# A decoder trunk layer on one core: the way from x to the first matrix product, written another way

## What is computed

```python
h = rmsnorm(x, norm_mix_g)          # x * rsqrt(mean(x*x) + eps) * g, over 2048 channels
p = h @ w_in                        # 2048 x 5120, columns [u_A | v_A | B_gate | C_gate | x_B]
v = rmsnorm(gelu(p[..., o1:o2]), sgu_norm_g)
y_a = gelu(p[..., :o1]) * chunk_sgu(v, w_s, b_s)
y_b = B_gate * causal_dwconv3(C_gate * x_B)
x = x + concat(GroupRMSNorm(y_a), GroupRMSNorm(y_b)) @ w_out
x = x + (silu(causal_dwconv3(h2 @ w_gate)) * (h2 @ w_up)) @ w_down    # h2 = rmsnorm(x)
```

## Time and profile before

| | |
|---|---|
| median of 3 runs | 2396.19 us (2394.45 to 2396.49) |
| the profiled execution | 2393.88 us, span 2392.2 us |
| PE busy in the span | 2339.3 us (98%) |
| DVE, ACT, POOL busy | 1331.8, 809.9, 269.0 us |
| first matmul of the first product | 34.99 us after the span's start |

### The profile page before, as it was taken

The page is one execution under the profiler, slowest core; times in us unless marked ns, Lnnn a source line. Parts: engine busy times, 40 slices in busy tenths (PEclk is TensorE's granted clock), DMA queues, the critical chain, the costliest instruction groups (busy, mean ns, idle before and its releaser), DMA issues.

```text
span 2392.2 us, 42851 instructions
## 1 busy us (share of the span) xinstructions
PE 2339.3 (98%) x17506; PEld 2328.4 (97%) x17506; DVE 1331.8 (56%) x1639; ACT 809.9 (34%) x1036; POOL 269.0 (11%) x362
## 2 busy tenths in 40 slices
PE   6999999999999899999999999999999999999996
PEld 5999999999999899999999999999999999999996
DVE  5347754455322767778778778778773222222332
ACT  6224322213111444444444444444442111111222
POOL 4310000000322000111111111111111000000111
PEclk7999999999999999999999999999999999999998
DMA  4522232323433233443443443443448543342222
GB/s 147 180 72 73 71 88 74 88 76 120 154 101 102 83 99 108 135 126 101 133 125 102 133 125 103 131 125 105 129 157 282 178 139 125 122 149 99 79 76 84
DMA packets 360461, 281.09 MB, mean 118 GB/s; under 512 B 8120, under 2 KB 348211, under 8 KB 355504
## 3 DMA queue, kind: packets, MB, share of 16 engines
q1 hardware_dynamic: 346960, 203.98, 29.5%
q0 software_dynamic: 13408, 75.76, 8.5%
HBM read 238.86 MB, written 40.85 MB: 117 GB/s over the span
## 4 chain that ended last, share of the span: by engine, by line
PE 95%; DVE 2%; ACT 1%; DMA 1%; POOL 0%; issue 0%; POOLq 0%; SPq 0%; DVEq 0%; ACTq 0%
PE ps L1535 19%; PE ps L1537 19%; PE ps L1536 19%; PE ps L1804 12%; PE ps L1806 12%; PE ps L1805 12%; DVE h_lo L1049 0%; DMA raw<-in_w_down_dram 0%; ACT ps L689 0%; DMA bias_b<-in_b_s_dram 0%; PE ps L1658 0%; ACT h_hi L661 0%; PE ps L1890 0%; PE ps L1671 0%; DMA x_nat<-in_x_prompt_dram 0%
## 5 line engine op out<-in xcount | busy, mean ns | idle before, releaser
L1535 PE MATMUL ps<-h_hi,w_hi 128*128 128x288 f32 x1792 | 533.0, 297 | 3.1 <-issue 2.0
L1023 DVE TENSOR_TENSOR w_lo<-raw,w_hi 128x1024 fp32r<-128x1024 f32 x216 | 270.2, 1268 | 467.9 <-ACT w_hi L640 258.9
L1536 PE MATMUL ps<-h_lo,w_hi 128*128 128x288 f32 x1792 | 529.5, 295 | 0.0
L1537 PE MATMUL ps<-h_hi,w_lo 128*128 128x288 f32 x1792 | 529.4, 295 | 0.0
L1535 PE MATMUL ps<-acts,w_hi 128*128 128x288 f32 x1408 | 415.5, 295 | 0.1
L1537 PE MATMUL ps<-acts,w_lo 128*128 128x288 f32 x1408 | 415.4, 295 | 0.0
L1536 PE MATMUL ps<-acts,w_hi 128*128 128x288 f32 x1408 | 414.6, 294 | 0.0
L1535 PEld LDWEIGHTS ps<-h_hi,w_hi 128*128 128x128 f32 x1792 | 337.8, 188 | 4.6 <-issue 2.7
L1536 PEld LDWEIGHTS ps<-h_lo,w_hi 128*128 128x128 f32 x1792 | 337.9, 189 | 0.0
L1537 PEld LDWEIGHTS ps<-h_hi,w_lo 128*128 128x128 f32 x1792 | 337.8, 189 | 0.0
L1804 PE MATMUL ps<-hq,w_hi 128*128 128x288 f32 x960 | 283.9, 296 | 0.0
(11 more groups left out here) (255 smaller groups left out, 4205.7 us busy)
## 6 DMA issues: line engine op xcount, KB each, us to landing
raw<-in_w_gate_dram SPq DMA_DIRECT2D x88, 512.0 KB, 4.6
raw<-in_w_down_dram SPq DMA_DIRECT2D x88, 512.0 KB, 3.4
raw<-in_w_in_dram SPq DMA_DIRECT2D x80, 512.0 KB, 4.5
act_scratch<-stage POOLq DMA_DIRECT2D x44, 576.0 KB, 3.0
acts<-act_scratch POOLq DMA_DIRECT2D x18, 1152.0 KB, 5.4
raw_c<-in_w_up_dram SPq DMA_DIRECT2D x40, 512.0 KB, 6.5
raw_d<-in_w_up_dram SPq DMA_DIRECT2D x40, 512.0 KB, 5.1
raw<-in_w_out_dram SPq DMA_DIRECT2D x32, 512.0 KB, 3.9
```

The source lines that it names most:

```text
L1023: v.tensor_tensor(w_lo[:, c % 4], raw[:, c % 2], w_hi[:, c % 4].bitcast(F32), ALU.subtract).then_inc(lo_ready, 1)
L1535: te.matmul(out, whi, xhi, start=start, stop=False)
L1536: te.matmul(out, whi, xlo, start=False, stop=False)
L1537: return te.matmul(out, wlo, xhi, start=False, stop=stop)
```

## The change

- The norm weight is multiplied straight from PSUM, no longer from X. ACT copies the bank to X after it has made h_hi.
- All h_lo subtractions are DVE's, each one unit behind the multiply. POOL has none.
- The first two weight tiles are both split early (pieces 2 and 3 behind the third block), and the first two tiles are done half by half: half 0 of tile 0, transposes of the sample block, half 0 of tile 1, half 1 of both. The diagonal sums stand after the first piece of tile 1's half 1, the late parameters' transposes in the middle of tile 2.
- Squares are written in place. ACT squares blocks 0, 1 and 2, DVE blocks 3 and 4 (`tensor_tensor_reduce`).
- The root and the reciprocal are taken on the 128x5 sums ahead of the diagonals. What PE spreads is the reciprocal root, and ACT copies it into rb.
- The store of X to the scratch is cut into four and stands ahead of the late parameter loads. The first two gelus wait for the first of the four only.
- SP loads x block 2 ahead of the first weight tile. x_nat4, ffnv and zpad lie elsewhere, and zpad's memset comes later.

The core of the diff:

```diff
-                if tb == 1:
+                if tb == 2:
                     tile2(w_in, HEADS, 0, first=True)
...
-            for tb in range(TB + 1):
-                n = P if tb < TB else SAMP
-                for kq in range(2):
-                    pool.wait_ge(xhi_ready, 4 * tb + kq + 1)
-                    g.tensor_tensor(h_lo[:, 4 * kq:4 * kq + 4, tb * P:tb * P + n], xg_of(kq, n),
...
             pool.wait_ge(x_t, 4 * (TB + 1))
-            pool.wait_ge(ssqn_ready, TB + 1)
+            for kq in range(4):
+                pool.wait_ge(xT_copied, 4 * TB + 1 + kq)
+                g.dma_start(scratch[:, 4 * kq * T:(4 * kq + 4) * T], X[:, 4 * kq:4 * kq + 4, :].rearrange("p k t -> p (k t)")
+                            ).then_inc(scratch_out0 if kq == 0 else scratch_out, 16)
+            pool.wait_ge(ssqn_ready, 3)
+            pool.wait_ge(ssqd_ready, 2)
             g.memset(acc[:, :], 0.0).then_inc(acc_done, 1)
+            g.memset(zpad[:, :], 0.0).then_inc(consts_ready, 1)
...
-            pool.wait_ge(xT_copied, 4 * (TB + 1))
-            g.dma_start(scratch, X[:, :, :].rearrange("p k t -> p (k t)")).then_inc(scratch_out, 16)
...
+            def x_square(tb):
+                n = P if tb < TB else SAMP
+                act.wait_ge(x_t, 4 * tb + 4)
+                a.activation(x_nat[tb][0:n, :], x_nat[tb][0:n, :], ACT.Square,
+                             accum_out=ssq_nat[0:n, tb:tb + 1]).then_inc(ssqn_ready, 1)
...
-                    act.wait_ge(x_t, u + 1)
+                    x_hi(u)
                     a.activation(X[:, 4 * kq:4 * kq + 4, tb * P:tb * P + n],
...
-                    if u >= 1:
-                        x_hi(u - 1)
                 if tb == 1:
                     for c in range(2):
                         split_hi(c, c)
...
+                elif tb == 2:
                     for c in range(2, 4):
                         split_hi(c, c)
...
+                elif tb == 3:
+                    x_square(0)
+                    x_square(1)
+            x_square(2)
+            act.wait_ge(ssqn_ready, 3)
+            act.wait_ge(ssqd_ready, 2)
+            a.activation(rms_nat, ssq_nat, ACT.Sqrt, bias=eps_t, scale=1.0 / DM).then_inc(nat_ready, 1)
+
+            act.wait_ge(ssq_done, 1)
+            act.wait_ge(xlo_ready, 4 * (TB + 1))
+            a.activation(rb[:, 0:SEQ], ps[:, SSQ_BANK, :], ACT.Copy)
+            a.activation(rb[:, SEQ:T], ssq_samp, ACT.Copy).then_inc(rms_ready, 1)
...
-                    v.tensor_tensor(xg_of(kq, n), X[:, 4 * kq:4 * kq + 4, tb * P:tb * P + n], gain,
+                    v.tensor_tensor(xg_of(kq, n), ps[:, 4 + kq, 0:4 * n].rearrange("p (k t) -> p k t", k=4), gain,
                                     ALU.mult).then_inc(xg_ready, 1)
+                    if u >= 1 and u != 12:
+                        x_lo(u - 1)
+                    if u in (8, 11):
+                        if u == 11:
+                            x_lo(u)
+                        split2_lo(0 if u == 8 else 2, 0 if u == 8 else 2)
+            x_lo(4 * TB + 3)
+            dve.wait_ge(consts_ready, 7)
+            for tb in range(TB - 1, TB + 1):
+                n = P if tb < TB else SAMP
+                v.tensor_tensor_reduce(x_nat[tb][0:n, :], x_nat[tb][0:n, :], x_nat[tb][0:n, :], 1.0, 0.0, ALU.mult, ALU.add,
+                                       ssq_nat[0:n, tb:tb + 1]).then_inc(ssqd_ready, 1)
...
+            dve.wait_ge(nat_ready, 1)
+            v.reciprocal(rms_nat, rms_nat).then_inc(rrms_ready, 1)
...
-            reciprocal_rms(1, rb)
-            dve.wait_ge(rrms_ready, 1)
-            dve.wait_ge(xlo_pool, 2 * (TB + 1))
+            dve.wait_ge(rms_ready, 1)
...
-            gemm(0, 0, 0, mid=rest_of_x)
-            pe.wait_ge(vec_ready, 3)
-            gemm(2, 2, 1, q1=spread_x_ssq, q3=params_t)
+            for half in range(2):
+                cols = slice(half * HALF, (half + 1) * HALF)
+                pe.wait_ge(xlo_ready, 4 * 3 if half == 0 else 4 * (TB + 1))
+                for tile in range(2):
...
+                        if half == 1 and c == 2:
+                            spread_x_ssq()
+                    if half == 0 and tile == 0:
+                        x_transposes(TB)
             for t in (2, 3):
                 pe.wait_ge(tile_read, t - 1)
-                gemm(2 * t, 2 * t, t % 2, mid=corner if t == 3 else None)
+                gemm(2 * t, 2 * t, t % 2, mid=params_t if t == 2 else corner)
```

More of the change, by code:

```diff
@@ L166, in build_layer @@
         out_nat = sb("out_nat", [P, TB + 1, DM], at=h_at)
+        x_nat.append(sb("x_nat4", [P, DM], at=zpad_at))
         rv = psq
@@ L1048, in x_lo @@
                 dve.wait_ge(xhi_ready, u + 1)
-                v.tensor_tensor(h_lo[at], xg_of(kq, n), h_hi[at].bitcast(F32), ALU.subtract).then_inc(xlo_dve, 1)
+                v.tensor_tensor(h_lo[at], xg_of(kq, n), h_hi[at].bitcast(F32), ALU.subtract).then_inc(xlo_ready, 1)
             dve.wait_ge(vec_ready, 1)
@@ L1629, in _ @@
             assert HALF <= 3 * P
-            pe.wait_ge(xlo_pool, 2 * 3)
-            pe.wait_ge(xlo_dve, 2 * 3)
-            gemm(0, 0, 0, mid=rest_of_x)
-            pe.wait_ge(vec_ready, 3)
-            gemm(2, 2, 1, q1=spread_x_ssq, q3=params_t)
+            for half in range(2):
+                cols = slice(half * HALF, (half + 1) * HALF)
+                pe.wait_ge(xlo_ready, 4 * 3 if half == 0 else 4 * (TB + 1))
+                for tile in range(2):
+                    if half == 0 and tile == 1:
+                        pe.wait_ge(vec_ready, 3)
+                    for s in range(2):
+                        c = 2 * tile + s
+                        if half == 0:
+                            pe.wait_ge(lo_ready, c + 1)
+                        for k in range(PK):
+                            kk = s * PK + k
+                            last = three(pair(tile, half), w_hi[:, c, k, :], w_lo[:, c, k, :],
+                                         h_hi[:, kk, cols], h_lo[:, kk, cols], kk == 0, kk == KT - 1)
+                        if half == 1:
+                            last.then_inc(piece_done, 1)
+                        if half == 1 and c == 2:
+                            spread_x_ssq()
+                    if half == 0 and tile == 0:
+                        x_transposes(TB)
             for t in (2, 3):
                 pe.wait_ge(tile_read, t - 1)
-                gemm(2 * t, 2 * t, t % 2, mid=corner if t == 3 else None)
+                gemm(2 * t, 2 * t, t % 2, mid=params_t if t == 2 else corner)
             with pe.Fori(2, HEADS // 2) as i:
```

85 lines of the change are left out of this document (32 added, 53 removed).

## The result

The change took **2380.98 us** (median of six runs, 2380.18 to 2383.49), the kernel before, in the same comparison, 2395.66 (six runs, 2394.45 to 2396.84): a ratio of 0.9942, interval 0.9932 to 0.9953. That is faster by 0.6%. Profile to profile the gain is 13.7 us (2393.88 to 2380.18), where the sum gave 10.0.

A forecast was written before the change was run, and what follows sets the result against it. PE, busy 2339.3 of 2392.2 us, bounds the kernel, so only its first product's start and holes count. -8.6 + 1.5 - 1.7 - 1.2 + 0.3 - 0.3 = -10.0 gave 2383.9 profiled, forecast 2386.2 us by median, range 2381.8 to 2391.4.

The forecast's parts named there:

- First product at 26.4: End of the prologue: PE's first product matmul starts at about 26.4 in place of 34.99 us, -8.6 us.
- a block's first multiply waits for POOL's two subtractions: Prologue loop of the kernel before: this wait sets the pace, with subtractions of 1.72 us (POOL), 1.37 and 1.75 (DVE).
- the same low-clock start of 5 us: PE at the first product: 5 us at the low clock as before, after only scattered transposes; no gain counted.
- Sample transposes: PE's stream behind half 0 of tile 0: the sample block's 16 transposes now stand there, +1.5 us.
- The hole ahead of the sums: PE ahead of the diagonal sums: the 1.74 us hole goes, -1.7 us.
- the low stretch behind it: PE behind the diagonal sums' hole: the low-clock stretch, 18 matmuls in 3.50 us, goes too, -1.2 us.
- a thin start: Tile 2: its weight split ends 3.5 us after the sums, where PE has 3.2 us of matmuls, +0.3 us.
- the parameters: Parameter transposes in the middle of tile 2: loads arrive just in time, the 0.32 us hole goes, -0.3 us.
- POOL's queue: Rival 1, tile 2: parameter loads behind the store come 3 us late, gain -5.8, 2390.4 us; chance 0.10.
- The squares: Rival 2, ahead of the diagonals: DVE's squares with sums take 4.6 us each, gain -7.8, 2388.4 us; chance 0.08.
- The subtraction: Rival 3, prologue: DVE's subtraction takes 1.5 us without POOL, within 2 us of no change, 2395; chance 0.06.
- The clock: Rival 4, first four half tiles: sample transposes keep PE at 1.2 GHz, +8.9 us, 2405.1 us; chance 0.04.

The follow-up runs named there:

- a4_pool_lo: The changed kernel with quarters 0 and 1 of every block's h_lo subtractions on POOL again: 2380.93 us, 0.9934 of the kernel before.
- c2_before_orders: The kernel before with sample transposes behind half 0 of tile 0 and DVE's subtractions one unit behind their multiplies: 2397.23 us, ratio 1.0007.
- d1_block_behind: The changed kernel with each DVE subtraction a whole block (four units) behind its multiply: 2391.93 us, 0.9984 of the kernel before.
- a1_sample_first: The changed kernel with the sample block's transposes ahead of the first product again: 2388.68 us, 0.9969 of the kernel before.
- b1_from_X: The changed kernel with the norm weight multiplied from X again and ACT's copy ahead of h_hi: 2386.37 us, 0.9958 of the kernel before.
- a2_gap: The changed kernel with the first product made to wait for all four lo pieces, a hole behind the transposes: 2386.17 us, 0.9955 of the kernel before.
- e1_fill: The changed kernel with idle PE time of the prologue filled by 31 unused identity transposes: 2381.00 us, 0.9938 of the kernel before.
- b4_act_squares: The changed kernel with all five squares on ACT and none on DVE: 2382.68 us, 0.9941 of the kernel before.
- c1_before_order: The kernel before with only the sample block's transposes moved behind half 0 of tile 0: 2406.70 us, ratio 1.0047.
- a3_tile_by_tile: The changed kernel with tile 0 done in both halves before tile 1: 2388.51 us, 0.9967 of the kernel before.
- b2_root_576: The changed kernel with root and reciprocal on 128x576 behind the spread sums again: 2389.21 us, 0.9973 of the kernel before.
- b3_store_behind: The changed kernel with the four stores of X behind the late parameter loads: 2382.73 us, 0.9946 of the kernel before.

## Why the prediction was right in direction and too small

**Bound and path: right.** PE fills the span, the gain came from an earlier first product and from holes that went, and all of it lies ahead of tile 2's end.

**First product at 26.4: 25.84.** The count by DVE's 0.61 per instruction holds to 0.6 us (third block split at 25.26 for 25.4, ACT's copy of unit 11 done at 25.03 for 25.3). But the reason beside it, one loop in which "a block's first multiply waits for POOL's two subtractions", is not what the trace of before shows. There no wait of a multiply ends with POOL; at the fourth block's start, for example, it ends with ACT's copy:

```profile
29.84 0.69 DVE L1065 TENSOR_TENSOR scaled<-X,vecs 128x512 f32<-128x512 f32 x1 [0.58 <-ACT X L669]
```

What POOL cost there was pace: two of DVE's six instructions for a block took some 1.38 and 1.75 us beside POOL instead of 0.68, 1.8 us for a block. With the multiply from PSUM, half of the subtractions can go back to POOL and the start is as early (a4_pool_lo). With the multiply from X and POOL's half kept, the two orders alone bring 28.77 (c2_before_orders). A kernel that is the change in all else but has both, X as operand and POOL's half, was not run, so the share of POOL's part in the earlier start is not shown. What is shown to hold the start is that a subtraction follows its multiply by one unit (d1_block_behind, +7.8), that the sample block's transposes stand behind (a1_sample_first, +8.1), and that the multiply doesn't wait for ACT (b1_from_X, +3.0).

**The step that failed** is this one: "I keep the same low-clock start of 5 us as in the earlier trace rows, since PE again has done only scattered transposes before it." They are not scattered where it counts: the last twelve stand back to back for 3.5 us and run into the product. A hole of 2.31 us there restores the slow start (a2_gap, 18), and with the idle time filled there is none (e1_fill). Five matmuls were slow instead of 21, 1.75 us that the sum had put at nothing. Part of the size is luck of this execution: the five other kernels, e1_fill apart, whose PE runs into the product without a hole had 7 to 15 slow, which makes the term 0.7 to 1.5. The range did allow for a clock that is up early, but hardly together with the smaller terms below: 13.5 below 2396.19 is 2382.7, and each of its printed ends lies another 1 us or so out, which no term explains.

**The other terms.** Sample transposes +1.13 for +1.5: mostly at the high clock. The hole ahead of the sums went (-1.7, as forecast), and the low stretch behind it was 15 matmuls, 1.6 us, for my 1.2. Tile 2 came at 54.7 without the 0.3 that I had added for a thin start, and the parameters without a wait. Start 0.6, clock 1.75, transposes 0.4, second low stretch 0.4 and tile 2 0.3 make 3.4 of the 3.7 us between 2383.9 and 2380.18; the rest is not traced. The forecast by medians added 2.3 for the distance of the profiled execution from the median of before; the change's stands 0.8 below its own, 1.5 more. Together that is the 5.2 from 2386.2 to 2380.98. That last 1.5 is no step of the mechanism: it depends on which executions were profiled. The change's was the fastest of its six, and the two slowest of the six, 2383.21 and 2383.49, lie inside the range.

**The rivals.** POOL's queue was not late (bias_b was issued at 48.4, PE took the parameters at 61.02 without waiting). The squares took 2.29 us, not 4.6. At 4.6 each the diagonals would have come at about 51.7, 1.6 us after PE wanted them (an estimate from 47.1 and 50.06), so that rival would have cost what it was priced at, a hole of 1 us or more; with ACT doing all squares there is no wait either (b4_act_squares). The rule in the Trainium skill, "Vector Engine (DVE) Microarchitecture Reference", section "Points that are easy to get wrong", speaks of the scalar_tensor_tensor family. The profile shows these squares as CUSTOM_DVE_ANT_0, so their row does not show whether the rule holds for that family. The subtraction is not slow of itself (0.68). The clock did not stay low through the sample block's transposes (1.00 from 30 to 34).

**What the parts are worth** does not add up. Taken out alone: sample order 7.7, half by half 7.5, root on five columns 8.2, DVE's order 10.9, PSUM operand 5.4, the store's place and ACT's squares under 2, POOL's part (with the multiply from PSUM) nothing; a sum of over 40 for a gain of 14.7 by medians. Each is one link of the same chain, and whichever is late makes PE stand and then run slow.

## What to carry to other kernels

A hole ahead of PE costs its length and often a slow stretch behind it (up to 24 matmuls here, 0.11 us each; none behind the 1.08 us of c2_before_orders, and behind the 1.97 us near 570 in half of the kernels); when a change brings or takes one, price both, and look at what PE does right ahead of a start, not at its mean load. In a prologue that several engines share, first ask what stands ahead of the last needed instruction on its own engine; the same instructions in another order were worth 8 us here, half of the subtractions on a helper engine nothing. And moving one engine's order without the others' can lose the gain at the next wait (c1_before_order, c2_before_orders).

## What the runs showed of the hardware

- The slow start differs from execution to execution. With the same PE stream up to there, the change had 5 slow matmuls, a3_tile_by_tile 7, b2_root_576 12, b3_store_behind 13 and b4_act_squares 13: up to 0.9 us that no edit explains. The clock's fall differs too: it is down to 0.50 from 17.0 us on in the change, and still 1.00 up to 20.5 in a3_tile_by_tile and b2_root_576. Behind the same hole of 1.97 us near 570 us the clock stayed at 2.4 GHz in some executions and fell to 1.2 in others. Why is open.
- With one large operand in PSUM, DVE's multiply and POOL's subtraction run side by side at 0.67 and 1.27 us (a4_pool_lo); with both in SBUF they take 1.76 and 1.71 (c2_before_orders).
- DVE squares 128x2048 with a sum in 2.29 us, read from SBUF and written there.
- A reciprocal on DVE of 128x576 takes 3.75 us, eight times a product of 128x288 from PSUM (0.46) for twice the columns.
